# Attention loop: the copy of step s-2's transposed probabilities before the exponential or bias of step s, on ScalarE and VectorE

## What is computed

```python
def banded_gqa(q, k, v, window, head_bias, sinks):
    def block(args):                        # 128 queries
        kb = lax.dynamic_slice_in_dim(kp, start, span, axis=1)
        vb = lax.dynamic_slice_in_dim(vp, start, span, axis=1)
        ...
        logits = jnp.einsum('btgrd,bsgd->bgrts', qi, kb) + bias
        p = masked_softmax(logits, mask, sink)
        return jnp.einsum('bgrts,bsgd->btgrd', p, vb)
```

## Time and profile before

| | |
|---|---|
| median of 3 runs | 1461.34 us (1461.04 to 1462.35) |
| the profiled execution | 1461.91 us, span 1460.2 us |
| TensorE matmul, weight load | 1436.3 us (98%), 1207.1 us (83%) |
| VectorE, ScalarE | 741.5 us (51%), 601.3 us (41%) |
| GpSimd | 112.4 us (8%) |
| attention loop, S(0) to the last T | 204.9 to 315.6 us |
| granted TensorE clock, mean | 0.995 |

### The profile page before, as it was taken

The page is one execution under the profiler, slowest core; times in us unless marked ns, Lnnn a source line. Parts: engine busy times, 40 slices in busy tenths (PEclk is TensorE's granted clock), DMA queues, the critical chain, the costliest instruction groups (busy, mean ns, idle before and its releaser), DMA issues.

```text
span 1460.2 us, 18290 instructions
## 1 busy us (share of the span) xinstructions
PE 1436.3 (98%) x6990; PEld 1207.1 (83%) x6990; DVE 741.5 (51%) x1200; ACT 601.3 (41%) x1009; POOL 112.4 (8%) x131
## 2 busy tenths in 40 slices
PE   6999999999999999999999999999999999999998
PEld 5788879998888888888888888888888888888887
DVE  6741677855665533556455444453457333333332
ACT  5633577755343332333333444532355333333221
POOL 5302322210000000000000111100000000000000
PEclk9999999999999999999999999999999999999999
DMA  9995200123433333312223233344332333333321
GB/s 283 322 237 186 75 1 2 31 73 93 152 101 109 98 97 101 101 44 87 68 63 87 58 87 101 87 144 113 89 90 84 115 89 101 99 93 94 110 79 57
DMA packets 227825, 149.71 MB, mean 103 GB/s; under 512 B 5330, under 2 KB 216014, under 8 KB 227108
## 3 DMA queue, kind: packets, MB, share of 16 engines
q1 hardware_dynamic: 223588, 131.63, 31.2%
q0 software_dynamic: 4160, 17.04, 4.0%
HBM read 140.92 MB, written 6.68 MB: 101 GB/s over the span
## 4 chain that ended last, share of the span: by engine, by line
PE 95%; SPq 1%; DMA 1%; DVE 1%; ACT 1%; issue 1%; DVEq 0%; ACTq 0%
PE ps L433 70%; PE ps L2215 6%; PE ps L2241 3%; PE ps L1938 3%; PE ps L2140 3%; PE ps L1830 3%; PE ps L2227 1%; DMA w_raw<-in_w_in_dram 1%; PE ps L1961 1%; PE ps L1899 1%; PE ps L2126 1%; PE ps L2125 1%; SPq L547 1%; PE ps L1954 1%; SPq L577 0%
## 5 line engine op out<-in xcount | busy, mean ns | idle before, releaser
L453 DVE TENSOR_TENSOR w_lo<-w_raw,w_hi 128x1024 fp32r<-128x1024 f32 (+1 forms) x214 | 258.1, 1209 | 251.0 <-ACT w_hi L448 248.1
L448 ACT ACTIVATE w_hi<-w_raw 128x1024 fp32r<-128x1024 f32 (+1 forms) x214 | 219.4, 1034 | 15.3 <-PE ps L433 11.3
L499 ACT ACTIVATE temps<-ps 128x512 f32<-128x512 f32 x67 | 40.0, 597 | 238.9 <-PE ps L433 238.9
L433 PE MATMUL ps<-g_hi,w_hi 128*128 128x512 f32 x384 | 95.8, 392 | 0.0
L433 PE MATMUL ps<-g_hi,w_lo 128*128 128x512 f32 x384 | 94.9, 389 | 0.0
L433 PE MATMUL ps<-g_lo,w_hi 128*128 128x512 f32 x384 | 94.8, 389 | 0.0
L433 PEld LDWEIGHTS ps<-g_hi,w_lo 128*128 128x128 f32 x384 | 72.1, 188 | 15.0
L433 PEld LDWEIGHTS ps<-g_lo,w_hi 128*128 128x128 f32 x384 | 72.1, 188 | 14.9
L433 PEld LDWEIGHTS ps<-g_hi,w_hi 128*128 128x128 f32 x384 | 71.5, 188 | 14.6
L433 PE MATMUL ps<-f_lo,w_hi 128*128 128x512 f32 x288 | 71.1, 389 | 0.0
L433 PE MATMUL ps<-f_hi,w_hi 128*128 128x512 f32 x288 | 71.1, 389 | 0.0
(11 more groups left out here) (442 smaller groups left out, 2734.8 us busy)
## 6 DMA issues: line engine op xcount, KB each, us to landing
w_raw<-in_w_in_dram SPq DMA_DIRECT2D x107, 512.0 KB, 3.9
w_raw<-in_w_ff_gate_dram SPq DMA_DIRECT2D x22, 512.0 KB, 3.8
w_raw<-in_w_ff_up_dram SPq DMA_DIRECT2D x22, 512.0 KB, 3.8
w_ada_shift_scale<-in_w_ada_dram SPq DMA_DIRECT2D x16, 512.0 KB, 7.8
w_raw<-in_w_r_out_dram SPq DMA_DIRECT2D x16, 512.0 KB, 4.5
w_raw<-in_w_ff_down_dram SPq DMA_DIRECT2D x16, 512.0 KB, 4.2
w_ada_gate<-in_w_ada_dram SPq DMA_DIRECT2D x4, 1024.0 KB, 10.9
x_spill<-x_t POOLq DMA_DIRECT2D x2, 2048.0 KB, 9.0
```

The costliest lines, as they stand in the source:

```text
L433: mm = pe.matmul(bank, w[:, slot, k], mov[:, at_k], start=first and n == 0 and k == 0, stop=last and n == 2 and k == kts - 1)
L448: act.activation(whi[:, slot, 0:kts], raw[:, slot, 0:kts], ACT.Copy).then_inc(hi_done, 1)
L453: nc.vector.tensor_tensor(wlo[:, slot, 0:kts], raw[:, slot, 0:kts], whi[:, slot, 0:kts].bitcast(F32), ALU.subtract).then_inc(lo_done, 1)
L499: act.activation(dst, ps[:, o % 4], func, scale=scale).then_inc(evac, 1)
```

## The change

On both engines the copy of step s-2 is written ahead of the instruction for step s. On ScalarE the weight conversion of step 61 moves ahead of the exponential too. All waits and all instructions stay.

```diff
--- before.py
+++ after.py
@@ -995,6 +995,15 @@
                 if s == 1:
                     act.wait_ge(m["vt_mm"], 3)
                     a.activation(proj[:, VA], ps[:, 4], ACT.Copy).then_inc(m["vt_ev"], 1)
+                t = s - 2
+                if 0 <= t < N_ATT and t % 2 == 1:
+                    act.wait_ge(m["t_mm"], t + 1)
+                    if t >= 2:
+                        act.wait_ge(m["pv_mm"], t - 1)
+                    w = att(t).width
+                    a.activation(pt[:, 1, 0:w], ps[:, 3, 0:w], ACT.Copy).then_inc(m["pt_a"], 1)
+                if s == CONVERT_AT:
+                    act_convert(act, None, 0, U_LAST + AHEAD)
                 if s < N_ATT:
                     G, n = divmod(s, 8)
                     act.wait_ge(m["s_bias"], s + 1)
@@ -1004,15 +1013,6 @@
                     a.activation(sc_of(s)[:, 0:w], sc_of(s)[:, 0:w], ACT.Exp, scale=-1.0,
                                  bias=row_min[:, G % 2, n:n + 1],
                                  accum_out=den[:, G % 2, att(s).head:att(s).head + 1]).then_inc(m["s_exp"], 1)
-                t = s - 2
-                if 0 <= t < N_ATT and t % 2 == 1:
-                    act.wait_ge(m["t_mm"], t + 1)
-                    if t >= 2:
-                        act.wait_ge(m["pv_mm"], t - 1)
-                    w = att(t).width
-                    a.activation(pt[:, 1, 0:w], ps[:, 3, 0:w], ACT.Copy).then_inc(m["pt_a"], 1)
-                if s == CONVERT_AT:
-                    act_convert(act, None, 0, U_LAST + AHEAD)
                 if s in K_WINDOW_AT:
                     k_round(2, K_WINDOW_AT.index(s))
                 G, n = divmod(s, 8)
@@ -1432,6 +1432,13 @@
             for s in range(STEPS):
+                t = s - 2
+                if 0 <= t < N_ATT and t % 2 == 0:
+                    dve.wait_ge(m["t_mm"], t + 1)
+                    if t >= 2:
+                        dve.wait_ge(m["pv_mm"], t - 1)
+                    w = att(t).width
+                    v.tensor_copy(pt[:, 0, 0:w], ps[:, 2, 0:w]).then_inc(m["pt_d"], 1)
                 if s < N_ATT:
                     u = att(s)
                     G = s // 8
@@ -1452,13 +1459,6 @@
-                t = s - 2
-                if 0 <= t < N_ATT and t % 2 == 0:
-                    dve.wait_ge(m["t_mm"], t + 1)
-                    if t >= 2:
-                        dve.wait_ge(m["pv_mm"], t - 1)
-                    w = att(t).width
-                    v.tensor_copy(pt[:, 0, 0:w], ps[:, 2, 0:w]).then_inc(m["pt_d"], 1)
                 if s < 2:
                     compressed_coefficients(s)
```

## The result

| | before | after |
| --- | --- | --- |
| median of 9 runs each, side by side | 1461.36 us | 1465.57 us (1464.71 to 1468.62) |
| after / before | | 1.003, 95% interval 1.0022 to 1.0038 |
| span of the profiled execution | 1460.2 us | 1466.9 us |
| loop, S(0) to S(95), same execution | 106.12 us | 111.37 us |

One of before's nine executions took 1605.86 us, with no cause on record, and the median without it is 1461.35.

A forecast was written before the change was run, and what follows sets the result against it. TensorE, 95% of the last-ending chain, bounds the kernel. Ring 4.4 plus restarts 0.9, less 3.2 given back and 0.3 in 128-wide steps, is +1.8 us: 1463.1 us, own range 1460.5 to 1465.2, stated range 1459.5 to 1467.5.

The forecast's parts named there:

- Rival 1: 128- and 256-wide part: TensorE's short waits bring three or four more low-clock stretches, 1466 to 1467 us; chance 0.25.
- Rival 2: VectorE, even steps: bias waits for the copy's end, about +4 us, 1467; chance 0.03.
- The ring: Even steps: cycle of transposes T(s-2), VectorE's copy, bias(s), scores S(s+2), T(s); 1.25 us at 256 columns, 4.4 us lost altogether.
- Zero both ways: Steps 24 to 27: low clock stays and hides the ring, or goes, winning 0.8 us that the ring takes; net zero.
- So it costs nothing: Combine now between an even and an odd step's bias: later scores are held to 3.92 us anyway, no cost.
- At 512: nothing lost: 512-wide steps: the ring takes 2.01 us against 2.11 available, 0.1 to spare, no loss.
- What it gives back: From step 28 on: twelve late products, 2.4 us, 3.6 with restarts; less 0.4 at step 61, 3.2 us won.
- The 128-wide steps: Steps before 24: twelve pairs fall from 20.05 to 19.8 us, 0.3 won; bounds -2.5 and +2.9.
- The signs: Loop stretches: 24.03 stays at 24 to 24.5, 28.55 grows 1.2, 34.86 grows 0.7, 20.05 unchanged; no product waits for ScalarE's copy.
- The restarts: TensorE, at scores that waited: 0.04 us each for 22 waits, 0.9 us lost; bounds 0 and 0.10 each.
- Rival 3: Early copies free TensorE and the ring, being shorter, does not bind: 1456 to 1458 us; chance 0.10.
- rival 4: Attention loop: order moves but gains and losses cancel, 1461.3 us; chance 0.12.

The follow-up runs named there:

- e2: Kernel before with only VectorE's copy of even steps moved first, ScalarE as before; 1470.05 us, ratio 1.0066.
- e4: ScalarE's copy first in all steps, VectorE's only from step 24 on, against the kernel before; 1464.76 us, ratio 1.0023.
- e6: Changed kernel plus one small VectorE copy (128x8) ahead of the copy on the seven even steps 34 to 46; 1465.61 us.
- e1: Kernel before with only ScalarE's copy of odd steps moved first, VectorE as before; 1457.64 us, ratio 0.9978.
- e3: The changed kernel itself, run once more for a second profile; 1465.27 us in its one execution.
- e10: e1 with all combines but the tenth and last moved behind the next step's bias, first-branch denominators with them; 1457.86 us, ratio 0.9978.
- e5: Changed kernel with the addition of the sinks replaced by adding a constant 1.0; 1465.76 us, ratio 1.0029.
- e9: Changed kernel with the sinks' addition and reciprocal moved one step later, behind that step's bias, for three query blocks; 1466.73 us, ratio 1.0043.
- e11: As e10, but of the first branch only group 3's denominators and combine are moved; 1456.69 us, ratio 0.9966.

## Why the prediction was right, and where it was wrong

- **The range held by luck.** The forecast's own range ended at 1465.2, and 1465.57 lies above it. The stated range reached to 1467.5 because rivals 1 and 2 had a share in it, and the runs bear out neither.
- **The ring** is right in form and in its own size. Its parts were forecast at 1.25 us and are 1.25; pairs forecast at 1.96 (band_b), 2.02 (band_a), 2.66 (384) and 3.48 (512) are 1.98, 2.04, 2.69 and 3.48. e2 and e4 show that it belongs to VectorE's half, e6 that it sets the pace.
- **The step that failed** is the count of what hangs on the ring: 5.3 us forecast, 7.3 measured. Three statements carry the difference. "Zero both ways" for steps 24 and 26: there the ring costs 1.0 us at full clock, and I had set it off against a low-clock stretch of one profile as if every execution had it; the profiles of e1, e3 and e4 do not show one. "So it costs nothing" of a combine between bias(e) and bias(o): where a product with the gate (L1505) follows at the next step, the two together push the copy of 30, 54 and 78, 0.43 more than forecast; and at 62 the combine of step 60 and the weight conversion of step 61 (1.22 us) do, 0.38 more. The second conversion, at step 63, costs nothing: pair 64 is a plain 2.69. "At 512: nothing lost": true of the five plain pairs, but pair 84 loses 0.55 because the combine behind the moved bias is what the output transposes wait for. With 46 (+0.16, open) and 0.15 at the hidden pairs that is 2.67; the gain at 36 and 38 against the forecast, 0.5, goes off it.
- **What it gives back** was forecast at 3.2 us from step 28 on and came out smaller. From S(28) to S(95) before takes 82.19 us and e1 79.39, so 2.8 are won. Of these 0.35 are at pair 62 (3.02 to 2.67), which the forecast did not count as won. Against that stands pair 36, up from 1.77 to 2.11, where the addition of the sinks now met GpSimd's subtraction. By the starts in before's trace eleven products are late and not twelve, together 2.36 us.
- **The 128-wide steps** were forecast at -0.3, with bounds of -2.5 and +2.9. Measured is +0.06: ScalarE's half -0.66, VectorE's +0.72. Right within 0.4, and both halves smaller than the bounds. (the earlier trace rows shows T(12) and copy(12), not T(13) and copy(14); the times read from it stand.)
- **The sum of the misses.** With the estimate of 0.8 for before's low clock, the loop grew by 4.1 us against 1.8 forecast. Of the 2.3 between them, 1.0 is the ring from step 28 on (6.3 measured, 5.3 forecast), 0.5 steps 24 and 26, 0.4 what is given back, 0.4 the 128-wide steps.
- **The signs** named ahead: the stretch of 24.03 us was to stay at 24 to 24.5 and is 24.49, that of 20.05 is 20.11, and that of 28.55 grew by 1.38 (1.2 forecast). The last stretch, cut at S(95), grew by 1.36 where 0.7 was forecast. Products that wait for ScalarE's copy did not vanish: two are left, 0.4 us.
- **The restarts** at a score were taken at 0.04; the plain 256-wide pairs came out 0.02 above the ring's rows. Smaller than forecast.
- **Rival 1, the clock**: one low-clock stretch in the loop of the changed kernel's first profile, none in its second nor in any experiment's. Where it came it cost 2.04 us, more than the 0.9 worked out, but it does not come three or four times, and the loop of the second profile, which has none, is 3.26 us longer than before's. So it is not what separates the medians.
- **Rival 2, the bias waits for the copy's end**: no. The bias starts 0.34 us behind the start of a copy of 0.42 us (245.01 and 244.67 above), also where the copy itself had waited. The Trainium skill, "VectorE: DVE Perf Modes", section "The DRAIN you can't avoid", lets the next instruction start when the pipe is empty and excepts those that are not held. On this pair the trace goes by the exception.
- **Rival 3, the ring does not bind**, is excluded by e6; **rival 4**, gains and losses cancel, by the interval.

## What to carry to other kernels

When a wait is moved in front of other work on one engine, write down the whole cycle that it closes, and then every other instruction that stands on that engine between its members: the plain cycle was right to 0.02 us here, and the 2 us by which the ring was undercounted lay at the irregular steps (the first of 256 columns, combine, gate product, weight conversion, output transposes). A change that touches two engines is two changes; run alone, one half was worth -3.2 us and the other +9. A low-clock stretch in one profile need not be a property of the program (the changed kernel had it in one profile of two), so no term of a sum should be set off against it.

## Hardware behaviour that I had not expected

VectorE's short addition SBUF to SBUF (128x8, normally 0.16 us) ended 0.01 to 0.03 us behind a GpSimd TENSOR_TENSOR wherever it started during one with more than its own 0.16 us left: 1.08 us (after, behind 240.55 + 1.28), 1.25 (e1), 1.02 (e10, behind w_lo), 1.09 already in the kernel before, at 261.41. With one input and a constant it was the same (e5). Started clear of GpSimd, it took 0.16 (e9, e11). A row w_lo x2 holds two subtractions of 1.27 us each: in e9 the addition started at 217.71, just as the first of such a row ended (216.44 + 1.27), and took 0.16 too. Instructions that read PSUM are not held: in the changed kernel the product with the gate at 234.97 takes its 0.69 us and the copy at 235.58 its 0.42, both started during a GpSimd addition (234.74 + 1.28). In e1, these rows show one case (GpSimd's and VectorE's):

```profile
234.64 1.28 POOL L768 TENSOR_TENSOR y_lo<-y_f,y_hi 128x512 fp32r<-128x512 f32 x1 [1.65 <-ACT y_hi L1024]
...
234.70 1.25 DVE L1477 TENSOR_TENSOR row_sum<-row_sum,sink_exp 128x8 f32<-128x8 f32 x1
```

In e1 pair 36 takes 2.11 us, where before, with the addition at 0.16, takes 1.77. e11 brought the pairs 36 and 38 down by 0.85 together, but it moved the reciprocal and the combine with the addition, so what the hold alone cost is not separated. The Trainium skill, "SBUF — State Buffer", section "Who interferes with whom", gives a rule: VectorE and GpSimd share one pair of SBUF ports under an exclusive lock, and whoever comes second is blocked for the other's whole instruction; VectorE needs the pair for two SBUF inputs and for the two-port modes, which a `tensor_scalar` can enter, but not with one SBUF input outside them. On these rows the trace agrees: all ends lie 0.01 to 0.03 us behind GpSimd's, both forms are held, and the copies, biases and products that read PSUM are free. That a port is the reason no run here shows by itself.
